# First modulation in column halves, and three weight splits moved, in a two-layer diffusion step on one core

## The chip, the core and the metric

The kernel runs on one core of a Trainium2 chip: TensorE (PE) multiplies, VectorE (DVE), ScalarE (ACT) and GpSimd (POOL) work on its inputs and results, and SyncE (SP) issues the transfers. The metric is the device time of one execution in microseconds (us), lower being better.

## The reference, cut to what matters

Two layers work on 512 latent tokens and 128 context tokens of width 1024. What this change touches is the first half of each layer's normalisation: `shift` and `scale` come from the conditioning, 1024 columns each, and every token is scaled by them before the first projection.

```
mod = (jax.nn.silu(cond) @ lp['w_ada'] + lp['b_ada'])[:, None, :]
sh1, sc1, g1, sh2, sc2, g2 = jnp.split(mod, 6, axis=-1)
h = rmsnorm(x, lp['norm1']) * (1 + sc1) + sh1
proj = h @ lp['w_in']
...
x = x + g1 * y
h = rmsnorm(x, lp['norm2']) * (1 + sc2) + sh2
u = conv3(h @ lp['w_up'], lp['conv_ff'])
```

## The kernel before, in words

Everything is written out by hand, engine by engine, with semaphores; each engine runs its list in order. The tokens lie transposed in `X`: eight tiles `t` of 128 model columns by 644 token columns. Matrices are multiplied in three products of rounded pieces: ScalarE makes the high part of a weight item (`W_hi`, function `item`), GpSimd the rest (`W_lo`, function `low`), and the tokens are split likewise into `H_hi` (ScalarE) and `H_lo` (VectorE). A weight item is 512 KB; there are three slots for raw items and three for split ones.

At a layer's start four things have to meet. **The norm**: ScalarE squares the eight tiles (`square`), VectorE adds them up in `SUM` as they come (`add_square`), TensorE sums over the columns (`first_sums` for `SUM`, `last_sums` for the last square), VectorE and GpSimd make the root (`roots`, `norm_root`), and TensorE spreads it over the partitions (`spread_roots`). **The modulation**: 16 items of `w_ada`, each 128 rows by 1024 columns, eight for `shift` and then eight for `scale`; TensorE multiplies each by the conditioning `CT`, four products of 256 columns that lie on four groups of 32 columns of the array (`ada_products`). Layer 0 takes the items from `AS0` with ten places, layer 1 from places that come free late in layer 0 (`BS_D`, `BS_H`, `BS_N`). When eight are done, ScalarE copies the row sums to `R` (`first_move`), TensorE turns them (`ada_rows`), and VectorE makes `MOD` and the gain `AB`. **The tiles**: for each tile VectorE makes `XN` (`normalise`), ScalarE scales it to `HF` with `MOD` and `AB` and makes `H_hi` (`modulate`), VectorE makes `H_lo` (`norm_rest`). **The first projection**: TensorE takes items 0 to 3 (512 columns, two tiles each, 30 products each), waiting for `H_lo` of each tile and for `W_lo` of each item.

The second norm of a layer does the same without such items in front: its modulation was made during the attention. There GpSimd scales the 128 context columns (`prompt_columns`), and ScalarE splits the third weight of the gated part, item 28 (`NPROJ + NOUT + 2`), between two of its tiles.

Of the kernel before, what the change touches and what calls it, by code (L numbers as in the profile page):

```python
# [313 lines left out]
def backbone_program(nc, x_prompt, x_sample, cache_mla_ckv, cache_mla_kpe, cache_gqa_k, cache_gqa_v,  # L314
# [5 lines left out]
    with ctx:  # L320
# [118 lines left out]
        const_in, c_in, f_in, mask_ok = sem("const_in"), sem("c_in"), sem("f_in"), sem("mask_ok")  # L439
# [40 lines left out]
        def staged(l, x):  # L480

            if l == 0:
                return AS0[:, x % NAS, :], as_in[x % NAS], 16 * (x // NAS + 1)
            return (BS_D[:, x, :] if x < 2 else BS_H[:, x - 2, :] if x < 12 else BS_N[:, x - 12, :]), bs_in[x], 16
# [187 lines left out]
        def _(sp):  # L672
            sp.dma_start(K[:, :], consts).then_inc(const_in, 16)
# [3 lines left out]
            sp.dma_start(CR[0:8, :], c.rearrange("a (k p) -> (a k) p", p=P)).then_inc(c_in, 16)  # L677
            sp.dma_start(CR[8:16, :], c_ctx.rearrange("(k p) -> k p", p=P)).then_inc(c_in, 16)
# [27 lines left out]
            def stage_ada(l, x):  # L706

                if l == 0 and x >= NAS:
                    sp.wait_ge(aw_used, x - NAS + 1)
                rows, landed_, _ = staged(l, x)  # L710
                sp.dma_start(rows, ada_src(l, x)).then_inc(landed_, 16)

            for l in range(DEPTH):
# [36 lines left out]
                if l == 0:  # L750
                    vectors()
                    for x in range(8 * ADA_A):
                        stage_ada(0, x)
                for r in range(NATTADA + NPROJ + NOUT):
# [27 lines left out]
                    if l and r == RAW - 1:  # L782
                        vectors()
                    if r == RAW:
# [42 lines left out]
                if l + 1 < DEPTH:  # L827

                    for x in range(NBS):
                        if x == 2:  # L830
                            sp.wait_ge(w_used, l * NW + (SPL + NW - 4))
                        if x == 12:
                            sp.wait_ge(x_pre, (l + 1) * KT)
# [14 lines left out]
        def _(pool):  # L848
# [6 lines left out]
            pool.wait_ge(const_in, 16)  # L855
# [14 lines left out]
            def prompt_columns(l, t):  # L870
# [5 lines left out]
                elif t == 0:  # L876
                    pool.wait_ge(mod_ok, l * 2 + 2)
# [4 lines left out]
            for l in range(DEPTH):  # L882
# [6 lines left out]
                for s in range(10, NPROJ):  # L889
                    item(l, s)  # L890
                rope_queries(nc.gpsimd, pool, l, 1)
# [7 lines left out]
                for s in range(NPROJ, NPROJ + NOUT + 2):  # L899
# [5 lines left out]
                for s in range(s0, s0 + 4):  # L905
# [11 lines left out]
        def _(act):  # L917
            def copy(dst, src):
# [6 lines left out]
                                 ACT.Silu).then_inc(c_silu, 1)  # L925

# [36 lines left out]
            def first_move(l, sc):  # L963

                act.wait_ge(aw_used, l * (8 * ADA_A) + 8 * sc + 8)
                if sc:
                    act.wait_ge(ada_tr, l * 3 + sc)
                copy(R[:, :], PS[:, sc, 0:256]).then_inc(ada_ev, 1)

            for l in range(DEPTH):  # L970
# [12 lines left out]
                first_move(l, 1)  # L983
                item(l, 0)
                act.wait_ge(mod_ok, l * 2 + 1)
                for t in range(KT):
                    modulate(l * 2, 0, t)
                    if t == 1:
                        item(l, 1)


                for ch in range(len(TOKEN_CHUNKS)):
                    mine = [s_ for s_, item_ in enumerate(TOKEN_ITEMS) if item_[0] == ch]
                    for s_ in mine[2 if ch == 0 else 1:]:
# [185 lines left out]
        def _(pe):  # L1180
# [8 lines left out]
            pe.wait_ge(const_in, 16)  # L1189
            for i in range(TT):  # L1190
# [8 lines left out]
            pe.wait_ge(c_in, 32)  # L1199
            tr(PS[:, 6, 0:16], CR[:, :]).then_inc(c_tr, 1)  # L1200
            pe.wait_ge(f_in, 16)
            tr(PS[:, 7, 0:KT], FR[:, :]).then_inc(f_tr, 1)
            pe.wait_ge(c_silu, 1)
# [3 lines left out]
            def ada_products(k, out, rows, first, last):  # L1207
# [3 lines left out]
                return ins  # L1211

# [56 lines left out]
            for l in range(DEPTH):  # L1269
# [11 lines left out]
                for x in range(8 * ADA_A):  # L1281
                    rows, landed_, value = staged(l, x)
                    pe.wait_ge(landed_, value)
                    ada_products(x % 8, PS[:, x // 8, 0:256], rows, x % 8 == 0, x % 8 == 7).then_inc(aw_used, 1)
                    if l and x == 5:
# [895 lines left out]
```

## Time and profile before

| what | before |
|---|---|
| median of 3 runs | 1748.97 us (1747.81 to 1749.28) |
| profiled execution | 1746.09 us |
| its span | 1744.1 us |
| mean granted TensorE clock | 0.989 of full |
| TensorE busy | 1668.3 us, 96% of the span |
| VectorE, ScalarE, GpSimd busy | 996.5, 590.2, 553.2 us |

The span is what the rows are counted in; 2.0 us of the execution lie around it. TensorE is busy nearly all of the time, so what can be won is where it waits, and it waits at the few places where a norm stands between two projections.

### The profile page before, as it was taken

What the parts mean: (1) busy time and instruction counts of PE and PEld (TensorE: products, weight loads), DVE (VectorE), ACT (ScalarE), POOL (GpSimd) and SP (SyncE); (2) the same over time, 40 slices, a digit from 0 to 9 for tenths busy, and PEclk for the clock granted to TensorE, in tenths of its full rate; (3) what the DMA queues carried; (4) which work ended last, traced back from release to release, by engine and by line L of the source; (5) the groups of instructions that cost most, each with busy time, mean ns of one, the idle gap of its engine ahead of it and who ended that gap; (6) DMA issues with size and microseconds to landing.
All of it is one profiled execution on the core that took longest, in us unless ns stands there. A gap on an engine that the chain in (4) does not pass through costs nothing.

```text
span 1744.1 us, 29770 instructions
## 1 busy us (share of the span) xinstructions
PE 1668.3 (96%) x11742; PEld 1507.7 (86%) x11742; DVE 996.5 (57%) x1604; ACT 590.2 (34%) x1085; POOL 553.2 (32%) x313
## 2 busy tenths in 40 slices
PE   6999988999999999999989999899999999999998
PEld 4888555798999999999968965568899999999997
DVE  4275455237766666666832844541476666666675
ACT  3423444425222222222352234452342222222224
POOL 1354010233433333443325510112333333333332
PEclk8999999999999999999999999999999999999999
DMA  8322520231222222222722344004122222222221
GB/s 325 105 76 79 182 76 1 87 120 49 84 74 72 72 72 72 72 73 73 268 54 80 97 127 149 24 13 157 49 62 79 77 72 72 72 73 79 77 73 61
DMA packets 148449, 156.17 MB, mean 90 GB/s; under 512 B 8280, under 2 KB 118404, under 8 KB 148356
## 3 DMA queue, kind: packets, MB, share of 16 engines
q1 hardware_dynamic: 148356, 154.87, 28.2%
q8 instruction: 66, 1.08, 0.3%
q14 instruction: 27, 0.22, 0.0%
HBM read 151.54 MB, written 3.31 MB: 89 GB/s over the span
## 4 chain that ended last, share of the span: by engine, by line
PE 84%; ACT 5%; DVE 5%; issue 2%; POOL 2%; DMA 1%; SPq 1%; ACTq 0%; DVEq 0%; POOLq 0%
PE PS L1182 79%; PE PS L1186 4%; ACT HF L947 1%; ACT PT L919 1%; POOL SS L887 1%; DMA AS<-in_w_ada_dram 1%; DVE H_lo L1754 1%; ACT PR L1055 1%; ACT H_hi L919 1%; POOL W_lo L859 1%; ACT W_hi L919 0%; DVE CF L2019 0%; DVE X L1780 0%; DVE XN L1747 0%; DVE CF L2022 0%
## 5 line engine op out<-in xcount | busy, mean ns | idle before, releaser
L859 POOL TENSOR_TENSOR W_lo<-RW,W_hi 128x1024 fp32r<-128x1024 f32 (+1 forms) x184 | 482.7, 2632 | 886.2 <-ACT W_hi L919 886.2
L1182 PE MATMUL PS<-H_hi,W_hi 128*128 128x384 f32 x1856 | 576.1, 310 | 10.8 <-DVE H_lo L1754 6.5
L1182 PE MATMUL PS<-H_hi,W_lo 128*128 128x384 f32 x1856 | 576.5, 311 | 0.0
L1182 PE MATMUL PS<-H_lo,W_hi 128*128 128x384 f32 x1856 | 576.0, 310 | 0.0
L1182 PEld LDWEIGHTS PS<-H_hi,W_hi 128*128 128x128 f32 x1856 | 351.7, 190 | 13.4 <-issue 9.5
L1182 PEld LDWEIGHTS PS<-H_hi,W_lo 128*128 128x128 f32 x1856 | 350.4, 189 | 0.0
L1182 PEld LDWEIGHTS PS<-H_lo,W_hi 128*128 128x128 f32 x1856 | 350.3, 189 | 0.1
L919 ACT ACTIVATE W_hi<-RW 128x1024 fp32r<-128x1024 f32 (+1 forms) x184 | 191.3, 1047 | 102.5 <-PE PS L1182 102.5
L1182 PE MATMUL PS<-G_hi,W_hi 128*128 128x384 f32 x704 | 218.8, 311 | 2.2 <-DVE G_lo L2032 2.2
L1182 PE MATMUL PS<-G_lo,W_hi 128*128 128x384 f32 x704 | 218.1, 310 | 0.0
L1182 PE MATMUL PS<-G_hi,W_lo 128*128 128x384 f32 x704 | 217.9, 309 | 0.0
L919 ACT ACTIVATE U<-PS 128x384 f32<-128x384 f32 (+1 forms) x176 | 67.2, 434 | 388.3 <-PE PS L1182 387.9
L2022 DVE SCALAR_TENSOR_TENSOR CF<-U,VT,CF 128x644 f32<-128x644 f32 x88 | 191.1, 2171 | 10.2 <-DVE CF L2019 2.4
L2017 DVE TENSOR_SCALAR CF<-U,VT 128x644 f32<-128x644 f32 x88 | 52.8, 600 | 240.2 <-ACT U L919 239.8
L2019 DVE SCALAR_TENSOR_TENSOR CF<-U,VT,CF 128x644 f32<-128x644 f32 x88 | 134.1, 1524 | 10.9 <-DVE CF L2017 3.7
L2045 DVE TENSOR_TENSOR DN<-PS,DN 128x384 f32<-128x384 f32 (+1 forms) x288 | 120.8, 477 | 26.2 <-PE PS L1182 26.2
L1182 PEld LDWEIGHTS PS<-G_hi,W_hi 128*128 128x128 f32 x704 | 132.8, 189 | 2.6 <-DVE G_lo L2032 2.6
L1182 PEld LDWEIGHTS PS<-G_hi,W_lo 128*128 128x128 f32 x704 | 133.7, 190 | 0.0
L1182 PEld LDWEIGHTS PS<-G_lo,W_hi 128*128 128x128 f32 x704 | 132.6, 188 | 0.0
L919 ACT ACTIVATE G_hi<-CF 128x644 fp32r<-128x644 f32 x44 | 32.7, 743 | 237.4 <-DVE CF L2028 237.4
L1182 PE MATMUL PS<-W_hi,H_hi 128*128 128x512 f32 (+1 forms) x240 | 90.8, 379 | 10.0 <-DVE H_lo L1754 7.4
L919 ACT ACTIVATE PT<-PS 128x512 f32<-128x512 f32 (+1 forms) x102 | 53.8, 576 | 109.9 <-PE PS L1186 105.7
(196 smaller groups left out, 1886.5 us busy)
## 6 DMA issues: line engine op xcount, KB each, us to landing
RW<-in_w_up_dram SPq DMA_DIRECT2D x88, 512.0 KB, 3.7
RW<-in_w_ada_dram SPq DMA_DIRECT2D x48, 512.0 KB, 4.0
RW<-in_w_down_dram SPq DMA_DIRECT2D x44, 512.0 KB, 3.6
RW<-in_w_in_dram SPq DMA_DIRECT2D x28, 512.0 KB, 3.7
AS<-in_w_ada_dram SPq DMA_DIRECT2D x16, 512.0 KB, 11.7
GS<-in_w_ada_dram SPq DMA_DIRECT2D x14, 512.0 KB, 6.9
BS_H<-in_w_ada_dram SPq DMA_DIRECT2D x10, 512.0 KB, 10.1
RW<-in_w_out_dram SPq DMA_DIRECT2D x32, 128.0 KB, 2.8
```

What stands on the lines that cost most here:

```text
L859: nc.gpsimd.tensor_tensor(W_lo[:, slot, 0:width], RW[:, raw, 0:width], W_hi[:, slot, 0:width].bitcast(F32), ALU.subtract).then_inc(w_lo, 1)
L887: nc.gpsimd.tensor_tensor(SS[:, 1, 0:40], SS[:, 0, 0:40], K[:, K_MH:K_MH + 40], ALU.pow).then_inc(hp, 1)
L919: return nc.scalar.activation(dst, src, ACT.Copy)
L947: nc.scalar.activation(HF[:, t % 2, c0:c1], XN[:, t % 2, c0:c1], ACT.Identity, bias=MOD[:, 24 * w + t, cond:cond + 1], scale=AB[:, w, t, c ...
L1055: nc.scalar.activation(prob_ap(step, u), score_ap(step, u), ACT.Exp, bias=stat(step, 0, u), scale=scale, accum_out=stat(step, 1, u)).then_ ...
L1182: return nc.tensor.matmul(out, lhsT, rhs, start=start, stop=stop, skip_group_check=True)
L1186: return nc.tensor.transpose(out, in_, K[0:n, K_ID:K_ID + n])
L1754: v.tensor_tensor(H_lo[:, t, :], HF[:, t % 2, :], H_hi[:, t, :].bitcast(F32), ALU.subtract).then_inc(h_lo, 1)
L2017: v.tensor_scalar(CF[:, ch, s, :], U[:, ch, s, 0:T], column(0), None, ALU.mult).then_inc(cv_own, 1)
L2019: v.scalar_tensor_tensor(CF[:, ch, s, :], U[:, ch, s, 1:T + 1], column(1), CF[:, ch, s, :], ALU.mult, ALU.add).then_inc(cv_own, 1)
L2022: v.scalar_tensor_tensor(CF[:, ch, s, :], U[:, ch, s, 2:T + 2], column(2), CF[:, ch, s, :], ALU.mult, ALU.add).then_inc(cv_done, 1)
L2045: ins = v.tensor_tensor(out, src, out, ALU.add)
```

## The change

It does five things.

1. The 16 items of the first modulation hold 256 rows by 512 columns now. The first eight give `shift` and `scale` of tiles 0 to 3 (half `h` = 0), the last eight those of tiles 4 to 7. A product has 128 columns instead of 256, and an item eight products instead of four (`first_products`).
2. TensorE takes the last eight (`late_products`) after the first projection item in layer 0, and before it in layer 1; `R` is copied and turned for each half apart, and VectorE makes `MOD` and `AB` for four tiles at a time (`first_modulation`). In layer 1 items 10 and 11 are the ones staged first, in `BS_D`.
3. In the list of the norm, the sums stand after the item x = 4 in layer 0 (after 8 before) and after x = 3 in layer 1 (after 1 before); `spread_roots` stands after the eight items. `normalise` of tile 1 moves behind the first `AB`.
4. ScalarE splits projection items 2 and 3 after tiles 3 and 5, no longer after tile 7, and item 28 between the last two squares of the second norm, no longer after its tile 4. GpSimd's list follows.
5. The constants come in five pieces, the identity first and the masks and tables last, behind the late items. The conditioning is loaded second and turned before the tokens, which wait for its Silu; `arrange_masks` moves to the end of the first norm.

```diff
@@ sync: start of the program @@
-            sp.dma_start(K[:, :], consts).then_inc(const_in, 16)
+            constant(K_ID, K_ID + P, const_in)
+            sp.dma_start(CR[0:8, :], c.rearrange("a (k p) -> (a k) p", p=P)).then_inc(c_in, 16)
+            sp.dma_start(CR[8:16, :], c_ctx.rearrange("(k p) -> k p", p=P)).then_inc(c_in, 16)
             for i in range(TT):
                 sp.dma_start(XIN[:, i, :], src).then_inc(x_in[i], 16)
-            sp.dma_start(CR[0:8, :], c.rearrange("a (k p) -> (a k) p", p=P)).then_inc(c_in, 16)
...
+                h, sc, kp = x // 8, x // 4 % 2, x % 4
+                src = w_ada[l, 2 * P * kp:2 * P * (kp + 1), D * sc + 512 * h:D * sc + 512 * (h + 1)]
+                sp.dma_start(rows.rearrange("p (k n) -> p k n", k=2),
+                             src.rearrange("(k p) n -> p k n", p=P)).then_inc(landed_, 16)
...
-                    for x in range(8 * ADA_A):
+                    for x in range(8):
                         stage_ada(0, x)
...
+                    elif r == RAW - 1:
+                        for x in range(8, 16):
+                            stage_ada(0, x)
+                        constant(K_MASK, K_ONE, rest_in)
+                        constant(K_SEL, K_MH, rest_in)
@@ gpsimd @@
-                for s in range(NPROJ, NPROJ + NOUT + 2):
+                for s in range(NPROJ, NPROJ + NOUT + 3):
                     item(l, s)
                 norm_root(l * 2 + 1)
@@ scalar @@
                 first_move(l, 0)
-                first_move(l, 1)
                 item(l, 0)
-                act.wait_ge(mod_ok, l * 2 + 1)
                 for t in range(KT):
+                    if t == 4:
+                        first_move(l, 1)
+                    if t % 4 == 0:
+                        act.wait_ge(mod_ok, l * 3 + 1 + t // 4)
                     modulate(l * 2, 0, t)
-                    if t == 1:
-                        item(l, 1)
+                    if t in (1, 3, 5):
+                        item(l, (t + 1) // 2)
...
                     if t == KT - 2:
                         item(l, NPROJ + NOUT + 1)
+                        item(l, NPROJ + NOUT + 2)
                 for t in range(KT):
                     modulate(l * 2 + 1, 1, t)
-                    if t == 4:
-                        item(l, NPROJ + NOUT + 2)
@@ tensor @@
             pe.wait_ge(const_in, 16)
+            pe.wait_ge(c_in, 32)
+            tr(PS[:, 6, 0:16], CR[:, :]).then_inc(c_tr, 1)
+
+            pe.wait_ge(c_silu, 1)
             for i in range(TT):
...
+            def first_products(l, x):
+                rows, landed_, value = staged(l, x)
+                pe.wait_ge(landed_, value)
+                h, sc, kp = x // 8, x // 4 % 2, x % 4
+                for kk in range(2):
+                    for g in range(4):
+                        ins = mm(PS[32 * g:32 * g + 32, 7 * h, P * sc:P * (sc + 1)], CT[:, 2 * kp + kk, :],
+                                 rows[:, 512 * kk + P * g:512 * kk + P * (g + 1)],
+                                 kp == 0 and kk == 0, kp == 3 and kk == 1)
+                ins.then_inc(aw_used, 1)
...
-                for x in range(8 * ADA_A):
...
+                for x in range(8):
+                    first_products(l, x)
+                    if l and x == 1:
                         pe.wait_ge(x_fin, l * KT + 6)
                         vector_rows()
-                    if x == (1 if l else 8):
+                    if x == (3 if l else 4):
                         first_sums(l * 2)
                         last_sums(l * 2)
...
+                spread_roots(l * 2)
+                ada_rows(l * 6, PS[:, 2, :]).then_inc(ada_tr, 1)
+
+                def late_products():
+                    for x in range(8, 16):
+                        first_products(l, x)
+                if l:
+                    late_products()
...
                     ins.then_inc(w_used, 1)
+                    if s == 0:
+                        if l == 0:
+                            late_products()
+                        pe.wait_ge(ada_ev, l * 6 + 2)
+                        rows_of(PS[:, 7, 256:512], R).then_inc(ada_tr, 1)
@@ vector @@
-                for t in range(2):
-                    normalise(N, t)
+                normalise(N, 0)
...
-            def norm_rest(N):
+            def norm_rest(N, middle=None):
+                normalise(N, 1)
                 for t in range(KT):
+                    if t == 4 and middle:
+                        middle()
                     dve.wait_ge(h_hi, N * KT + (t + 1))
...
+            def first_modulation(l, h):
+                src = PS[:, 7, 256:512] if h else PS[:, 2, 0:256]
+                dve.wait_ge(ada_tr, l * 3 + h + 1)
+                bias = VT[:, 0:16].rearrange("p (o x g b) -> p o x g b", o=2, x=2, b=1)[:, :, h]
...
+                dve.wait_ge(mod_raw, l * 2 + h + 1)
+                gains(0, 4 * h, 4)
...
-                for sc in range(ADA_A):
...
-                gains(l, 0)
-                norm_rest(l * 2)
+                first_modulation(l, 0)
+                norm_rest(l * 2, lambda: first_modulation(l, 1))
+                if l == 0:
+                    arrange_masks()
```

TensorE's list in layer 0, from the first modulation item (`AS,CT`) to the first product of the projection (`W_hi,H_hi`), before. An `x36` counts products, four to an item; `K,NS` is the spread and `K,R` the turned row sums:

```order
L1182 MATMUL PS<-AS,CT 32x256 x36
L1182 MATMUL PS<-K,SUM 128x1 x5
L1182 MATMUL PS<-K,SQ 128x1 x5
L1182 MATMUL PS<-AS,CT 32x256 x12
L1182 MATMUL PS<-K,NS 128x128 x5
L1182 MATMUL PS<-AS,CT 32x256 x4
L1186 MATMUL PS<-K,R 128x128 x2
L1182 MATMUL PS<-AS,CT 32x256 x12
L1186 MATMUL PS<-K,R 128x128 x2
L1182 MATMUL PS<-W_hi,H_hi 128x512
L1182 MATMUL PS<-W_lo,H_hi 128x512
```

The same place after; behind the line of dots stands the end of the first projection item. The `x40` of `32x128` counts products, eight to an item:

```order
L1202 MATMUL PS<-AS,CT 32x128 x40
L1202 MATMUL PS<-K,SUM 128x1 x5
L1202 MATMUL PS<-K,SQ 128x1 x5
L1202 MATMUL PS<-AS,CT 32x128 x24
L1202 MATMUL PS<-K,NS 128x128 x5
L1206 MATMUL PS<-K,R 128x128 x2
L1202 MATMUL PS<-W_hi,H_hi 128x512
...
L1202 MATMUL PS<-W_hi,H_lo 128x512
L1202 MATMUL PS<-AS,CT 32x128 x64
L1206 MATMUL PS<-K,R 128x128 x2
L1202 MATMUL PS<-W_hi,H_hi 128x512
```

Half of the products have left the stretch ahead of the projection, and stand behind its first item in twice the number of pieces.

ScalarE's list in layer 0 from the copy of the row sums, before, through the first four tiles (each is two `HF` and one `H_hi`; rows of further tiles read alike and are left out):

```order
L919 ACTIVATE R<-PS 128x256 x2
L919 ACTIVATE W_hi<-RW 128x1024
L947 ACTIVATE HF<-XN,MOD,AB 128x512
L947 ACTIVATE HF<-XN,MOD,AB 128x128
L919 ACTIVATE H_hi<-HF 128x644
L947 ACTIVATE HF<-XN,MOD,AB 128x512
L947 ACTIVATE HF<-XN,MOD,AB 128x128
L919 ACTIVATE H_hi<-HF 128x644
L919 ACTIVATE W_hi<-RW 128x1024
L947 ACTIVATE HF<-XN,MOD,AB 128x512
```

and after, from its second weight split to the third and on to the copy of the second half's sums:

```order
L937 ACTIVATE W_hi<-RW 128x1024
L966 ACTIVATE HF<-XN,MOD,AB 128x512
L966 ACTIVATE HF<-XN,MOD,AB 128x128
L937 ACTIVATE H_hi<-HF 128x644
L966 ACTIVATE HF<-XN,MOD,AB 128x512
L966 ACTIVATE HF<-XN,MOD,AB 128x128
L937 ACTIVATE H_hi<-HF 128x644
L937 ACTIVATE W_hi<-RW 128x1024
L937 ACTIVATE R<-PS 128x256
L966 ACTIVATE HF<-XN,MOD,AB 128x512
```

The split of item 2 has moved between the tiles, and the copy to `R` for the second half stands before the fifth tile, so that ScalarE waits there for TensorE's late products.

GpSimd's list around the root of the second norm (`NS`), before and after in one piece each:

```order
L638 TENSOR_TENSOR QS<-TC,TD 128x4x32 x2
L859 TENSOR_TENSOR W_lo<-RW,W_hi 128x1024 x10
L867 TENSOR_TENSOR NS<-NS,K 128x5
L878 TENSOR_SCALAR HF<-XN,AB,MOD 128x128 x8
L859 TENSOR_TENSOR W_lo<-RW,W_hi 128x1024 x4
```

```order
L639 TENSOR_TENSOR QS<-TC,TD 128x4x32 x2
L876 TENSOR_TENSOR W_lo<-RW,W_hi 128x1024 x11
L884 TENSOR_TENSOR NS<-NS,K 128x5
L895 TENSOR_SCALAR HF<-XN,AB,MOD 128x128 x8
L876 TENSOR_TENSOR W_lo<-RW,W_hi 128x1024 x3
```

One split of a weight has passed from behind the eight context pieces (`HF`) to ahead of the root.

## Rows read from the trace of the kernel before

**Rows 1.** Timeline of layer 0's start: start us, duration us, engine, line, operation, idle before.
```profile
9.40 4.87 DVE L1691 COPY X<-PS 128x512 f32<-128x512 f32 x8 [0.16 <-PE PS L1186]
13.23 1.28 ACT L924 ACT_TABLE_LOAD   x1 [13.23 <-PE PS L1186]
14.60 1.36 ACT L939 ACTIVATE SQ<-X 128x644 f32<-128x644 f32 x2
...
17.69 4.56 DVE L1723 TENSOR_TENSOR SUM<-SUM,SQ 128x644 f32<-128x644 f32 x5 [0.87 <-ACT SQ L939]
...
23.28 0.64 PE L1182 MATMUL PS<-AS,CT 128*32 128x256 f32 x8 [0.22 <-DMA AS<-in_w_ada_dram]
...
25.11 1.27 PE L1182 MATMUL PS<-K,SUM 128*128 128x1 f32 x10
...
28.39 2.79 PE L1182 MATMUL PS<-AS,CT 128*32 128x256 f32 x24
...
31.11 2.34 PE L1182 MATMUL PS<-K,NS 128*128 128x128 f32 x10
...
34.09 0.28 DVE L1748 TENSOR_TENSOR XN<-X,PS 128x128 f32<-128x128 f32 x1
...
37.22 1.20 ACT L947 ACTIVATE HF<-XN,MOD,AB 128x512 f32<-128x512 f32 x2
...
40.47 0.76 PE L1182 MATMUL PS<-W_hi,H_hi 128*128 128x512 f32 x1 [3.71 <-DVE H_lo L1754]
...
57.03 0.50 PE L1182 MATMUL PS<-W_hi,H_hi 128*128 128x512 f32 x1 [1.08 <-POOL W_lo L859]
```

**Rows 2.** Timeline of layer 1's start, TensorE and one row of ScalarE.
```profile
874.27 1.07 PE L1182 MATMUL PS<-BS_D,CT 128*32 128x256 f32 x16
876.30 1.28 PE L1182 MATMUL PS<-K,SUM 128*128 128x1 f32 x10 [0.96 <-DVE SUM L1723]
...
880.40 2.50 PE L1182 MATMUL PS<-K,NS 128*128 128x128 f32 x10
...
889.64 0.44 PE L1186 MATMUL PS<-K,R 128*128 128x128 f32 x2 [0.50 <-ACT R L919]
...
890.53 1.20 ACT L947 ACTIVATE HF<-XN,MOD,AB 128x512 f32<-128x512 f32 x2
...
893.78 0.76 PE L1182 MATMUL PS<-W_hi,H_hi 128*128 128x512 f32 x1 [3.71 <-DVE H_lo L1754]
...
910.35 0.50 PE L1182 MATMUL PS<-W_hi,H_hi 128*128 128x512 f32 x1 [1.04 <-POOL W_lo L859]
```

**Rows 3.** Timeline of layer 0's second norm.
```profile
389.40 2.40 POOL L859 TENSOR_TENSOR W_lo<-RW,W_hi 128x1024 fp32r<-128x1024 f32 x1 [7.99 <-ACT W_hi L919]
...
395.32 1.18 POOL L867 TENSOR_TENSOR NS<-NS,K 128x5 f32<-128x5 f32 x1 [3.53 <-DVE NS L1731]
...
408.95 1.05 ACT L919 ACTIVATE W_hi<-RW 128x1024 fp32r<-128x1024 f32 x1
...
412.40 0.44 PE L1182 MATMUL PS<-H_hi,W_hi 128*128 128x384 f32 x1 [0.40 <-DVE H_lo L1754]
...
417.31 0.44 PE L1182 MATMUL PS<-H_hi,W_hi 128*128 128x384 f32 x1 [1.09 <-DVE H_lo L1754]
```

**Rows 4.** Timeline of TensorE, 172.7 to 178.6: products of 128 columns on two groups (128*64).
```profile
172.71 0.88 PE L1182 MATMUL PS<-PT,PMG 128*64 128x128 f32 x12
...
177.91 0.66 PE L1182 MATMUL PS<-PT,PMG 128*64 128x128 f32 x8
```

**Rows 5.** Timeline of TensorE, 399.25 to 399.30 alone: what begins in 0.05 us.
```profile
399.26 0.42 PE L1182 MATMUL PS<-GS,CT 128*32 128x256 f32 x4
```

**Rows 6.** Windows: stretch, its length, busy us and instructions by engine, granted clock, DMA.
```profile
28.40:33.40 5.00, 5.00 (x38) 3.15 (x37) 0.17 (x1) 0.00 (x0) 1.17 (x1) 0.53 1.03 406
```

**Rows 7.** The page's DMA issues: count, KB each, median us from issue to landing.
```profile
RW<-in_w_ada_dram SPq DMA_DIRECT2D x48, 512.0 KB, 4.0
RW<-in_w_in_dram SPq DMA_DIRECT2D x28, 512.0 KB, 3.7
```

More of the change, by code:

```diff
@@ L827, in _ @@
                 if l + 1 < DEPTH:
[L829 to L833, printed above, removed]
+                    for x in (10, 11):
+                        stage_ada(l + 1, x)
+                    sp.wait_ge(w_used, l * NW + (SPL + NW - 4))
+                    for x in range(10):
+                        stage_ada(l + 1, x)
+                    sp.wait_ge(x_pre, (l + 1) * KT)
+                    for x in range(12, NBS):
                         stage_ada(l + 1, x)
@@ L904, in _ @@
                 s0 = NPROJ + NOUT + 2
-                for s in range(s0, s0 + 4):
+                for s in range(s0 + 1, s0 + 4):
                     item(l, s)
@@ L961, in ada_move, with first_move @@
                 copy(R[:, :], PS[:, 7, 0:256]).then_inc(ada_ev, 1)
[L963 to L968, printed above, removed]
+            def first_move(l, h):
+                act.wait_ge(aw_used, l * (8 * ADA_A) + 8 * h + 8)
+                if h:
+                    act.wait_ge(ada_tr, l * 3 + h)
+                copy(R[:, :], PS[:, 7 * h, 0:256]).then_inc(ada_ev, 1)
             for l in range(DEPTH):
@@ L1280, in _ @@
                     pe.wait_ge(x_fin, l * KT + 5)
-                for x in range(8 * ADA_A):
[L1282 to L1285, printed above, removed]
+                for x in range(8):
+                    first_products(l, x)
+                    if l and x == 1:
                         pe.wait_ge(x_fin, l * KT + 6)
                         vector_rows()
-                    if x == (1 if l else 8):
+                    if x == (3 if l else 4):
                         first_sums(l * 2)
                         last_sums(l * 2)
-                    if x == (4 if l else 11):
-                        spread_roots(l * 2)
-                    if x == 12:
-                        ada_rows(l * 6, PS[:, 2, :]).then_inc(ada_tr, 1)
-                ada_rows(l * 6 + 1, PS[:, 4, :]).then_inc(ada_tr, 1)
+                spread_roots(l * 2)
[5 more added lines that the diff above has]
+                    late_products()
                 def w_ready(s):
@@ L1696, in _, with arrange_masks @@
             v.memset(X[:, :, T - 2:T], 0.0).then_inc(setup_v, 1)
-            lower, upper = K[:, K_MASK:K_MASK + P], K[:, K_MASK + P:K_MASK + 2 * P]
-            copy(K[:, K_MASK + 3 * P:K_MASK + 4 * P], upper).then_inc(mask_ok, 1)
-            dve.wait_ge(mask_ok, 1)
-            copy(upper, lower).then_inc(mask_ok, 1)
-            dve.wait_ge(mask_ok, 2)
-            v.memset(lower, 0.0).then_inc(mask_ok, 1)
-            dve.wait_ge(mask_ok, 3)
+            def arrange_masks():
+                dve.wait_ge(rest_in, 32)
+                lower, upper = K[:, K_MASK:K_MASK + P], K[:, K_MASK + P:K_MASK + 2 * P]
+                copy(K[:, K_MASK + 3 * P:K_MASK + 4 * P], upper).then_inc(mask_ok, 1)
+                dve.wait_ge(mask_ok, 1)
+                copy(upper, lower).then_inc(mask_ok, 1)
+                dve.wait_ge(mask_ok, 2)
+                v.memset(lower, 0.0).then_inc(mask_ok, 1)
+                dve.wait_ge(mask_ok, 3)
             for n in range(2 * TT):
@@ L1983, in _ @@
                                         ALU.subtract).then_inc(y_lo, 1)
-                gains(l, 1)
+                filled(dve, l, ("AT", 4))
+                gains(1, 0, KT)
                 for t in range(KT):
```

44 lines of the change are left out of this document (22 added, 22 removed).

## The prediction

> **What bounds the kernel now.** I read the page's busy times first: TensorE works 96% of the span, so a change can win only where TensorE waits. The waits of TensorE then lead to four places: the start of each layer and the second norm of each layer. At each I read the timeline, engine beside engine.
>
> In layer 0 TensorE's own order sets the start. `SUM` is complete at 17.69 + 4.56 = 22.25, but the sums stand behind the item x = 8 and begin at 25.11; the items before them come one at a time from memory (x = 7 starts at 23.28 after waiting for its transfer). The spread starts at 31.11, the first tile of `XN` is there at 34.37, and `HF` still waits until 37.22 for the second half of the modulation; the first projection product runs at 40.47, 3.25 after `HF` [rows 1]. In layer 1 all items are on the chip, and TensorE walks the list itself: a wait of 0.96 for `SUM`, the spread at 880.40, the last turned row sums at 889.64 after a wait of 0.50, `HF` at 890.53, the first product at 893.78 [rows 2]. About 15 us after each first product stands a wait of 1.08 and 1.04 for the `W_lo` of item 2 [rows 1, 2]. In the second norm TensorE waits 0.40 and 1.09 for `H_lo` of late tiles, behind ScalarE's split of item 28 at 408.95 (1.05) [rows 3]; layer 1 repeats it.
>
> **The price of an item.** This one number carries the sum, so first that. Two old items in a row take 1.07, one takes 0.64: 0.43 for an item [rows 1, 2]. It holds eight instructions (each product is two), 54 ns each. The four products on the four groups begin within 0.05 us and run together [rows 5], so an item is two such rounds of about 0.215. In attention, twelve and eight instructions of 128 columns on two groups take 0.88 and 0.66: 55 ns each, 110 for a pair that runs together [rows 4]. A new item holds sixteen instructions of 128 columns. If rounds of four take as long as these pairs, it is 4 × 0.11 = 0.44, no more than before. If an instruction costs 55 ns however many groups share the array, it is 16 × 55 ns = 0.88. Rows 5 shows four starting far closer together than 55 ns, so I take 0.48, with 0.43 and 0.88 as ends. In the stretch where the granted clock was 0.53 [rows 6], three items took 2.79, so 0.93 each [rows 1]; I keep that for items that lie there.
>
> The Trainium skill ("TensorE: Matmul & The Clock Gate", Back-to-back issue gap) speaks against the change: in a stream of weight loads and products it gives about 81 ns for a product of 128 columns, which I'd estimate as 16 × 81 ns = 1.30 for a new item. The trace disagrees already, with 54 and 55 ns in such streams; the sum by the page is with the rivals.
>
> **Layer 0, before the first product.** ScalarE's squares begin at 14.60, after Silu, while the tokens are complete at 9.40 + 4.87 = 14.27 [rows 1]. With Silu done ahead of the tokens the squares start up to 0.33 earlier, and `SUM` ends at about 21.92. But the tokens now wait for Silu, and Silu needs the conditioning, its turn and the table load of 1.28 [rows 1]; no row shows how these land when they are issued second. I bound the start of the squares by 1.0 to either side of the value taken, less than one table load. The items come at 406 GB/s [rows 6], 0.52 MB in 1.29 us, so x = 4 is there three items before 23.28, at 19.4, and the sums no longer wait for it. They take 25.11 to 28.39, 3.28, at a low clock: 21.95 to 25.25. Items 5 to 7 follow in 2.8: the spread begins at 28.05. `XN` of the first tile ended 3.26 after the spread began [rows 1]: 31.3. The row sums are copied during the spread and turned right behind it; `MOD` and `AB` come about 0.45 after (889.64 + 0.44 to 890.53 in layer 1 [rows 2]), so `HF` starts at about 31.75 and the first product at 35.0: **5.5 sooner**.
>
> **Layer 0, what is given back.** The late products now stand behind item 0, in TensorE's full stream: 8 × 0.48 = **3.84 later**. Behind them TensorE waits for ScalarE's copy of `R`, 0.50 and 0.44 as at 889.64 [rows 2], **1.0 later**. Queued behind that wait is item 1; ScalarE waits before tile 4 in turn, and GpSimd behind it. Tile 4 is not needed until item 2: the late products end at about 46.6, the copy and turn at 47.55, `H_lo` of tile 4 some 3.7 later at 51.3, and item 2 starts at about 55.3, so this is covered by 4 us. The late transfers, eleven after x = 7 with the three raw weights among them, land at 23.3 + 11 × 1.29 = 37.5, before item 0 ends at about 42.8 (items 0 and 1 took 40.47 to 55.95, 57.03 less the wait [rows 1], so 7.75 each). The wait for `W_lo` goes, since item 2 is split after tile 3: **1.08 sooner**. Layer 0: −5.5 − 1.08 + 3.84 + 1.0 = **−1.7**.
>
> **Layer 1.** The sums stand behind x = 3, so `SUM` is there: 0.96 less. Ahead of the spread there are three items more, 1.44, and the vector rows: from the end of the spread at 882.90 to the wait at 889.14, 6.24 hold eleven items (4.7), turned rows (0.44) and these vector rows, at most 1.1; I take 0.6. The spread begins at 880.40 − 0.96 + 1.44 + 0.6 = 881.5 and ends at 884.0 with its 2.50 [rows 2]; turned rows to 884.4, `HF` at 884.9, the first product at 888.1. The eight late products, 3.84 from 884.4, end at 888.3 and now decide by a hair: 5.5 sooner. The wait of 1.04 goes, 0.44 of turned rows comes behind item 0; `R` for them is copied under that item. Layer 1: **−6.1**. Low clock at the first product (0.76 against 0.50 at 910.35 [rows 2]) could be less with TensorE busy right up to it; I leave that to the range, 1 us.
>
> **Second norms.** The split of item 28 (1.05) moves to where ScalarE waits for the residual. GpSimd's part of it comes behind the one that starts at 389.40, so 389.40 + 2.40 + 2.40 = 394.2, ahead of the root at 395.32 [rows 3]: hidden, by 1.1; with that cover gone each norm would be later by what is over. Both waits go, 0.40 + 1.09 = 1.5 in each layer: **−3.0** (−0.6 to −3).
>
> **Sum.** −1.7 − 6.1 − 3.0 = −10.8. The profiled execution of before was 1746.09 (its span 1744.1 and 2.0 around it), 2.9 under the median of the runs, so it would become 1735.3, and the median 1748.97 becomes **1738.2**. The other edits (order of the constants, masks at the end of the first norm, places of the staged items) cost nothing in it: they lie on the transfer queue behind the items or behind VectorE's work on the norm, and GpSimd waits for them only after its splits of the first projection.
>
> **Rivals.** *A, the item's price follows the number of instructions*, 0.88: 0.40 more for each item. Layer 0 has eleven on the path, x = 5 to 7 at the low clock (2.8 more) and the late eight (3.2 more); layer 1 sixteen (6.4 more). Sum −10.8 + 12.4 = +1.6: 1750.6, no change that can be told. For it: 54 and 55 ns are nearly the same price at 256 and 128 columns. Against it: rows 5. By the skill's 81 ns, an estimate, another 0.42 per item would give about 1762; this is in the chance of the slower side.
> *B, slower: the late transfers*. They read rows of 2 KB in place of 4 KB, and TensorE stands behind item 0 until they land. At the rate of rows 6 they have 42.8 − 37.5 = 5.3 to spare. The 14.2 us of transfers would have to take 14.2 + 5.3 + 10.8 = 30.3 for before's time, a rate of 0.47, and at a third, 42.6, the kernel ends 12 us later: 1761. Against it: weights of the projection, in rows of 2 KB and less, land in 3.7, those of 4 KB in 4.0 [rows 7].
> *C, the second norms gain nothing*, because ScalarE's last square or the root waits for the moved split: −7.8, 1741.2. For it: only 1.1 of cover; the trace has no row of that meeting.
>
> **How the numbers follow.** Forecast 0.62, A 0.13, B and the page's price together 0.11, C 0.14. About 0.2%, 3.5 us, is what a measurement of this kernel can tell from no change. Faster: 0.62 + 0.14 = 0.76; same 0.13; slower 0.11. The range begins at 1734 (items at 0.43, squares 1.0 sooner, 1 us of clock in layer 1, and the scatter of the runs) and reaches to 1746.5, which holds C, squares 1.0 later, and an item price up to about 0.7.
>
> **What would show it.** In layer 0: sums at about 22, spread at about 28, first product near 35, then 128 instructions of late products in about 3.9, a short wait for `R`, and no wait for `W_lo` at item 2. In layer 1 the first product some 14 us after the first item where it was 19.5 (874.27 to 893.78), and no wait ahead of it for `H_lo` above 1 us. In the second norms no wait of TensorE for `H_lo`. The forecast is wrong if an item takes over 0.8, if TensorE waits for a transfer behind item 0, or if the root of a second norm starts later after the last residual.

## The result, and the profile after

| what | after | before, beside it |
|---|---|---|
| median of 5 runs | 1738.11 us (1733.82 to 1739.49) | 1748.97 us (1746.68 to 1749.64) |
| ratio, 95% interval | 0.9939 (0.9926 to 0.9951) | |
| again, on another chip, 6 runs | 1737.55 us, ratio 0.9933 (0.9917 to 0.9948) | 1748.09 us |
| profiled execution, span | 1739.49 us, 1737.3 us | 1746.09 us, 1744.1 us |
| mean granted TensorE clock | 0.987 | 0.989 |
| TensorE busy | 1671.3 us | 1668.3 us |

The kernel is 10.9 us faster by the medians, where 10.8 was forecast. The two profiled executions lie only 6.6 apart: that of before is below all five of its times, that of after is the slowest of its five. So the forecast's total can't be read off the two traces; each of its steps can, and one has to ask each time whether the row is the program's or that execution's. Two executions below (one of the kernel before, one of a variant) took 2057 and 2226 us with a mean granted clock of 0.75 and 0.68, and are left out of every median here.

Layer 0's start after, by the timeline (start us, duration us, engine, line, operation, idle before), answers to [rows 1]:

```profile
15.21 1.37 ACT L958 ACTIVATE SQ<-X 128x644 f32<-128x644 f32 x2 [10.20 <-DVE X L1731]
...
18.31 4.56 DVE L1767 TENSOR_TENSOR SUM<-SUM,SQ 128x644 f32<-128x644 f32 x5 [0.86 <-ACT SQ L958]
...
22.93 2.29 PE L1202 MATMUL PS<-K,SUM 128*128 128x1 f32 x10 [2.44 <-DVE SUM L1767]
25.08 2.27 PE L1202 MATMUL PS<-K,SQ 128*128 128x1 f32 x10
27.29 2.79 PE L1202 MATMUL PS<-AS,CT 128*32 128x128 f32 x48
30.00 2.50 PE L1202 MATMUL PS<-K,NS 128*128 128x128 f32 x10
...
36.94 0.76 PE L1202 MATMUL PS<-W_hi,H_hi 128*128 128x512 f32 x1 [4.00 <-DVE H_lo L1800]
...
45.42 3.70 PE L1202 MATMUL PS<-AS,CT 128*32 128x128 f32 x128
49.63 0.44 PE L1206 MATMUL PS<-K,R 128*128 128x128 f32 x2 [0.50 <-ACT R L937]
```

The order of things is the forecast one: TensorE now waits for `SUM` (2.44), the first product comes at 36.94 where it came at 40.47, the eight late items stand behind item 0, and no wait for `W_lo` follows. 128 instructions take 3.70: 29 ns each, 0.46 an item. The two sums, which took 3.28 with the item ahead of them busy [rows 1], take 4.36 here behind an idle TensorE. The windows of the same trace (length; busy us and instructions of TensorE, its weight loads, VectorE, ScalarE, GpSimd; granted clock; DMA) show the clock: 0.95 while TensorE hardly works (0.07 of 2.00), then 0.50, the lower of the two levels at which the rows run:

```profile
21.00:23.00 2.00, 0.07 (x1) 0.07 (x1) 1.69 (x5) 1.70 (x5) 0.00 (x0) 0.95 1.02 383
23.00:25.00 2.00, 2.00 (x10) 2.00 (x10) 0.00 (x0) 0.12 (x1) 0.00 (x0) 0.50 1.05 407
25.00:27.00 2.00, 2.00 (x11) 2.00 (x11) 0.17 (x1) 0.00 (x0) 0.00 (x0) 0.50 1.05 408
```

Layer 1's start, the same view, answers to [rows 2]:

```profile
872.02 1.08 PE L1202 MATMUL PS<-BS_H,CT 128*32 128x128 f32 x32
...
874.65 1.28 PE L1202 MATMUL PS<-K,SUM 128*128 128x1 f32 x10
875.79 1.96 PE L1202 MATMUL PS<-K,SQ 128*128 128x1 f32 x10
877.68 3.64 PE L1202 MATMUL PS<-BS_H,CT 128*32 128x128 f32 x64
881.25 2.19 PE L1202 MATMUL PS<-K,NS 128*128 128x128 f32 x10
...
888.22 0.47 PE L1202 MATMUL PS<-W_hi,H_hi 128*128 128x512 f32 x1 [0.92 <-DVE H_lo L1800]
```

The wait for `SUM` is gone and the first product stands 16.2 after the first item, against 19.5 before. Four items at 877.68 took 3.64, twice the price: a low clock again (0.50 in the windows from 877 to 881). The product itself takes 0.47, not 0.76: TensorE was busy up to 0.92 ahead of it, and the windows give 1.00 from 885 on.

GpSimd in the second norm of layer 0, ScalarE's moved split, and the one product of TensorE that still waits there, answer to [rows 3]:

```profile
389.17 2.40 POOL L876 TENSOR_TENSOR W_lo<-RW,W_hi 128x1024 fp32r<-128x1024 f32 x1 [7.99 <-ACT W_hi L937]
...
391.56 1.06 ACT L937 ACTIVATE W_hi<-RW 128x1024 fp32r<-128x1024 f32 x1 [2.46 <-PE PS L1202]
...
392.69 2.36 POOL L876 TENSOR_TENSOR W_lo<-RW,W_hi 128x1024 fp32r<-128x1024 f32 x1 [1.12 <-ACT W_hi L937]
395.10 1.19 POOL L884 TENSOR_TENSOR NS<-NS,K 128x5 f32<-128x5 f32 x1
...
402.72 0.41 PE L1202 MATMUL PS<-H_hi,W_hi 128*128 128x384 f32 x1 [1.75 <-DVE H_lo L1800]
```

The waits of 0.40 and 1.09 are gone; the one of 1.75 for the first tile was there before too, at 402.95. The root starts at 395.10 where it started at 395.32, and this whole stretch is 0.22 earlier, so it is not delayed; but the moved piece ends at 392.69 + 2.36 = 395.05, and the cover, the time by which it is done ahead of the root, is 0.05.

### The profile page after: what moved, and what is told of

Read it like the earlier page. It is cut to its first block, busy times and chain, and to the rows that moved or that the text cites. A ratio compares the mean times of both kernels' runs of the same rounds, so it can differ in the third digit from the quotient of the medians.

```text
span 1737.3 us, 30288 instructions
## 1 busy us (share of the span) xinstructions
PE 1671.3 (96%) x11998; PEld 1520.9 (88%) x11998; DVE 999.0 (58%) x1606; ACT 590.7 (34%) x1085; POOL 554.5 (32%) x313
## 4 chain that ended last, share of the span: by engine, by line
PE 88%; DVE 5%; ACT 4%; issue 2%; POOL 1%; DMA 0%; SPq 0%; ACTq 0%; DVEq 0%
PE PS L1202 84%; PE PS L1206 5%; ACT PT L937 1%; ACT PR L1076 1%; POOL SS L904 1%; DVE CF L2072 0%; DVE X L1833 0%; ACT H_hi L937 0%; DVE CF L2075 0%; DVE HO L2017 0%; DVE SUM L1767 0%; ACT HO L937 0%; POOL W_lo L876 0%; DMA XIN<-in_x_sample_dram 0%; ACT PMM L937 0%
## 5 line engine op out<-in xcount | busy, mean ns | idle before, releaser
L2075 DVE SCALAR_TENSOR_TENSOR CF<-U,VT,CF 128x644 f32<-128x644 f32 x88 | 191.0, 2171 | 10.2 <-DVE CF L2072 2.4
L2070 DVE TENSOR_SCALAR CF<-U,VT 128x644 f32<-128x644 f32 x88 | 48.9, 555 | 240.8 <-ACT U L937 240.4
L2072 DVE SCALAR_TENSOR_TENSOR CF<-U,VT,CF 128x644 f32<-128x644 f32 x88 | 138.9, 1578 | 10.3 <-DVE CF L2070 2.4
```

The source lines that it names most:

```text
L2070: v.tensor_scalar(CF[:, ch, s, :], U[:, ch, s, 0:T], column(0), None, ALU.mult).then_inc(cv_own, 1)
L2072: v.scalar_tensor_tensor(CF[:, ch, s, :], U[:, ch, s, 1:T + 1], column(1), CF[:, ch, s, :], ALU.mult, ALU.add).then_inc(cv_own, 1)
L2075: v.scalar_tensor_tensor(CF[:, ch, s, :], U[:, ch, s, 2:T + 2], column(2), CF[:, ch, s, :], ALU.mult, ALU.add).then_inc(cv_done, 1)
```

## The experiments

Medians are given with the ratio to the kernel before on the same chip and its 95% interval. "Faster than the changed kernel" is by its 1738.11 and 1737.55.

**Item 28 alone.** In the kernel before:

```diff
...
                         item(l, NPROJ + NOUT + 1)
+                        item(l, NPROJ + NOUT + 2)
...
-                    if t == 4:
-                        item(l, NPROJ + NOUT + 2)
```

> The kernel before, with only the split of item 28 moved between the last two squares and GpSimd's share ahead of the root. Theory of the prediction: both waits of TensorE in each second norm go (0.40 and 1.09, 0.40 and 1.07) and nothing comes in their place, so 3.0 us less than before and a root that starts where it did, 3.5 us after the start of the last residual add. Rival C: the root or the last square comes later by what GpSimd still has to do, the gain is under 1 us, and the row of the root shows it.

1747.04 against 1749.36, ratio 0.9987 (0.9978 to 0.9996): 2.3 us faster, 0.7 to 3.8. Its trace shows no wait of TensorE for `H_lo` after the first tile, and its GpSimd rows the root right behind the moved piece:

```profile
396.18 2.36 POOL L859 TENSOR_TENSOR W_lo<-RW,W_hi 128x1024 fp32r<-128x1024 f32 x1 [1.12 <-ACT W_hi L919]
398.58 1.19 POOL L867 TENSOR_TENSOR NS<-NS,K 128x5 f32<-128x5 f32 x1
```

The mechanism holds and rival C falls, though "3.5 after the last residual add" now rests on 0.04 of cover. The 3.0 is within the interval. By the rows each norm gives 2.0 (see the second norms in the account below).

**The changed kernel without item 28's move.** Only that move, taken back.

> The changed kernel with only item 28's split back behind tile 4 of the second norms. Theory: the waits of 0.40 and 1.1 come back in both layers, 3.0 us slower than the changed kernel (about 1741), the same as the move was worth alone. Rival: with the other moves it is worth something else, under 1 or over 5 us.

1743.42, ratio 0.9960 (0.9946 to 0.9974). The kernel before had 1749.95 on this chip, more than on the others, so the ratios compare better than the medians: 0.9960 against 0.9939 and 0.9933 is 3.7 to 4.7 us slower than the changed kernel (5.3 and 5.9 by the medians alone). TensorE's timeline has the two waits again:

```profile
414.01 0.44 PE L1203 MATMUL PS<-H_hi,W_hi 128*128 128x384 f32 x1 [0.40 <-DVE H_lo L1801]
...
418.91 0.44 PE L1203 MATMUL PS<-H_hi,W_hi 128*128 128x384 f32 x1 [1.08 <-DVE H_lo L1801]
```

The waits are back as the theory says, and the interval holds its 3.0; the rows make it 2.0 in each layer.

**Splits of items 2 and 3 alone.** In the kernel before:

```diff
-                    if t == 1:
-                        item(l, 1)
+                    if t in (1, 3, 5):
+                        item(l, (t + 1) // 2)
...
```

> The kernel before, with only the splits of items 2 and 3 moved behind tiles 3 and 5. Theory of the prediction: the waits of 1.08 and 1.04 for the low part of item 2 go, 2.1 us faster, and it is the halves that make the splits' old place cost 4.5 in each layer (as seen with the splits put back). Rival: ScalarE's tiles come later by the two splits between them, TensorE waits for H_lo of a late tile instead, and less than 1 us is won.

1749.93 against 1749.95, ratio 0.9996 (0.9985 to 1.0007). In the trace the wait of 1.08 ahead of item 2 is gone, no wait for a late tile has come, and TensorE's wait for `ST` in attention, at 191.94 before, comes at 190.78, 1.16 earlier. So the rival's mechanism is not there in layer 0; but the median does not show the 2.1, and the interval (2.6 faster to 1.2 slower) leaves both theories standing on size. In that execution the root of the second norm comes at 397.99, 2.67 later than before's 395.32; the windows between show a clock of 0.97 where the execution of before had 1.00:

```profile
200.00:300.00 100.00, 89.60 (x722) 56.21 (x719) 50.78 (x122) 43.89 (x122) 7.93 (x27) 0.97 0.21 65
300.00:360.00 60.00, 55.80 (x429) 45.77 (x427) 17.35 (x33) 25.23 (x53) 11.82 (x5) 0.97 0.33 115
```

**All splits back.** The changed kernel with both moves undone (the two diffs above, backwards).

> The changed kernel with all three weight splits back in their old places (items 2 and 3 after tile 7, item 28 after tile 4 of the second norm). If the parts add up as in the prediction's sum, this is 2.1 + 3.0 = 5.1 us slower than the changed kernel, with the waits of about 1 us for the low part of item 2 back in both layers and those of 0.4 and 1.1 in both second norms. Rival: in layer 0 TensorE has the late products between items 0 and 1, which gives ScalarE time, so the wait for item 2 does not come back there and the loss is about 4.

1754.60 against 1749.36, ratio 1.0031 (1.0019 to 1.0042): slower than before. Neither theory had this size. TensorE's timeline has the waits, in both layers:

```profile
62.55 0.50 PE L1203 MATMUL PS<-W_hi,H_hi 128*128 128x512 f32 x1 [4.47 <-POOL W_lo L876]
...
916.59 0.79 PE L1203 MATMUL PS<-W_hi,H_hi 128*128 128x512 f32 x1 [4.49 <-POOL W_lo L876]
```

ScalarE's fifth tile waits for the late modulation, so tile 7, and the split behind it, come later: at 59.03, where the kernel before split at 53.48. The wait for item 2 was 1.08; with halves and the old place it is 4.47, and 4.49 in layer 1, where ScalarE's fifth tile likewise starts after a wait for `AB` (2.06 at 905.59). The parts don't add up: without the moved splits the halves bring waits of 9.0. By the ratios (1.0031 against 0.9960 with item 28 alone put back) the splits of items 2 and 3 are worth 12.4 here; what the rest of it is was not taken apart.

**Old order of loads.** The constants in one piece and the conditioning behind the tokens again:

```diff
-            constant(K_ID, K_ID + P, const_in)
+            constant(0, K_N, const_in)
...
-            pe.wait_ge(c_silu, 1)
             for i in range(TT):
```

> The changed kernel with the constants in one piece, the conditioning behind the tokens and its Silu behind the transposes, as before; the masks stay at the end of the norm. In the changed kernel the squares started at 15.21, not at 14.27 as forecast. Theory: that is the new order's doing (first transposes at 5.36 on a slow TensorE, a wait of 0.75 for the second token tile); here the squares start at about 14.6 again and the kernel is about 0.6 us faster than the changed one, with the first product near 36.3. Rival: something else in the changed kernel holds the tokens, the squares stay at 15.2, and Silu behind them makes this 0.3 us slower.

1738.55, ratio 0.9932 (0.9919 to 0.9945): the same. The squares started at 14.86, but that decides nothing: in ten traces with the new order they start between 13.99 and 16.29 (15.21, 14.83, 14.81, 14.86, 16.29, 14.84, 14.47, 13.99, 14.43, 14.96), in four with the old one between 14.60 and 14.86. Their means are 14.87 and 14.75: the new order brings no earlier start, and more scatter.

**Sums after x = 6 in layer 0.**

```diff
-                    if x == (3 if l else 4):
+                    if x == (3 if l else 6):
```

> The changed kernel with the sums of layer 0 after the item x = 6 in place of x = 4. In the changed kernel TensorE waited 2.44 us for SUM behind x = 4, and then took sums (4.36), three items (2.79) and spread (2.50) all at a granted clock of 0.50. Theory: the position is the sized-wrong step; the items x = 5 and 6 fill the wait, the sums start at about 23.2, run at a higher clock in 2.5 to 3.3, and the spread starts near 27.5 in place of 30.0, so the first product comes 2 to 2.5 us sooner, about 34.6. Rival: the clock falls in the sums whatever stands ahead of them, sums and x = 7 take as long as before, and the spread starts within 1 us of 30.0.

1737.89, ratio 0.9933 (0.9921 to 0.9946): no difference by the median. In the trace:

```profile
23.52 0.64 PE L1202 MATMUL PS<-AS,CT 128*32 128x128 f32 x16 [1.40 <-DMA AS<-in_w_ada_dram]
24.09 1.28 PE L1202 MATMUL PS<-K,SUM 128*128 128x1 f32 x10
25.23 1.89 PE L1202 MATMUL PS<-K,SQ 128*128 128x1 f32 x10
27.05 1.08 PE L1202 MATMUL PS<-AS,CT 128*32 128x128 f32 x16
28.77 2.50 PE L1202 MATMUL PS<-K,NS 128*128 128x128 f32 x10 [0.64 <-POOL NS L884]
```

The first sums are back at 1.28 and both take 2.96 in place of 4.36, with no wait for `SUM` ahead of them. But x = 6 landed late, the spread begins 1.2 sooner, not 2.5, and 0.35 of that is the squares' earlier start. Half of the theory holds; its price does not. With the same position in the two runs with x = 6 and late products ahead, the sums took 1.28 and 1.25 once and 2.29 and 2.27 once, and the old order, where TensorE comes to the sums busy, has the long ones too, in the run with item 28 alone:

```profile
24.83 1.08 PE L1181 MATMUL PS<-AS,CT 128*32 128x256 f32 x8 [0.18 <-DMA AS<-in_w_ada_dram]
25.84 2.29 PE L1181 MATMUL PS<-K,SUM 128*128 128x1 f32 x10
28.00 2.27 PE L1181 MATMUL PS<-K,SQ 128*128 128x1 f32 x10
```

Over all fourteen traces: in the seven in which TensorE waits for `SUM` (0.81 to 3.39) the sums take 2.29 and 2.27 every time, though in two of these the items ahead of the wait ran at the low level already (1.08 each); in the other seven the first sums take 1.27 or 1.28 four times and 2.29 three times. So filling the wait does not always keep the clock, and that the wait lowers it is not shown.

**Late products of layer 1 behind item 0.**

```diff
-                if l:
-                    late_products()
...
-                        if l == 0:
-                            late_products()
+                        late_products()
```

> The changed kernel with the late products of layer 1 behind its first projection item, as in layer 0. Theory: ahead of it they cost nothing, since TensorE waits there for the first tile anyway; behind it they stand in the full stream. The first product stays within 0.5 us of 16 us after the first item, and the kernel is 3.7 us slower by the products, plus up to 1.5 for a first item at low clock. Rival: they do set the first product, which then comes about 2 us sooner, so the loss is under 2 us.

1743.68, ratio 0.9966 (0.9957 to 0.9976): about 5.6 to 6.1 us slower than the changed kernel. The rows:

```profile
888.11 0.77 PE L1202 MATMUL PS<-W_hi,H_hi 128*128 128x512 f32 x1 [5.32 <-DVE H_lo L1797]
...
901.21 0.44 PE L1206 MATMUL PS<-K,R 128*128 128x128 f32 x2 [0.50 <-ACT R L937]
```

The first product waits 5.32 for the first tile where the late products had stood, 13.77 after the first item and not the 16 expected; the changed order has it at 13.80 too where its clock held (the run with x = 6). So ahead of the first product they cost nothing, and behind item 0 their 3.7, a low-clock first item (0.77) and a new wait of 0.50.

**Late products of layer 0 ahead of item 0.** The late items are loaded four behind each of the first two raw weights:

```diff
...
-                if l:
-                    late_products()
+                late_products()
...
-                        if l == 0:
-                            late_products()
```

> The changed kernel with the late products of layer 0 ahead of the first projection item, as in layer 1, and the late items loaded between the raw weights (four behind the first, four behind the second). Theory: in layer 0 the change won little because 3.70 of late products and 0.94 of waiting and turning stand in the full stream, while TensorE waits 4.00 ahead of the first product; there the products fit, the first item no longer runs at a low clock, and the first product comes no more than 0.5 later: 3.5 to 5 us faster than the changed kernel. Rival B in a new place: the late items land after 36.9, TensorE waits for them, and nothing is won or the kernel is slower.

1734.92 (1729.44 to 1737.21), ratio 0.9917 (0.9898 to 0.9935): 2.6 to 3.2 us faster than the changed kernel by the medians, with intervals that overlap. The first product came at 38.18, 1.24 later than in the changed kernel and not the 0.5 at most, after waits for the last two transfers (0.68 and 0.63 at 36.34 and 37.61), and TensorE's wait for `ST` in attention at 187.23, against 191.68 and 192.09 in the two traces of the changed kernel. That row has the 3.5 to 5 of the theory, the medians have less; a little of rival B is there too.

> As the run before, with the sums of layer 0 after x = 6. Theory: the sums after x = 6 bring the first product about 1 to 1.5 us sooner in the trace, and the late items, whose landing does not move, then decide: at most 1 us faster than the run before. Rival: with the sums later TensorE uses items later, places come free later and the late items land later: slower than the run before.

1730.79 over 4 runs, ratio 0.9892 (0.9874 to 0.9911): 4.1 faster than the run before by the medians, where at most 1 was expected. And once more:

> The kernel with all eight late products ahead of the first product of layer 0 and the sums after x = 6 once more, since its first median stands on few times and the version with five of them ahead was not faster than it. Theory: 7 us under the changed kernel was partly the clock; in the trace layer 0 is 2.6 us ahead of it at the first products of the attention, so a ratio to the kernel before of 0.990 to 0.992. Rival: 0.989 or less again, so the gain is the program's.

1733.57 over 4 runs, ratio 0.9904 (0.9887 to 0.9920). The theory's 0.990 to 0.992 holds it. The wait for `ST` stands at 189.05 and 187.00 in these two, no sooner than the 187.23 without x = 6, so no row of layer 0's start answers to the 4.1. These medians lie 4 to 7 us under the changed kernel's and 16 to 17 under before's; whether x = 6 adds to what the place of the late products brings is not settled.

**Five ahead, three behind.** As the last kernel, but `late_products` takes x = 8 to 12 ahead of the first product and the rest behind item 0.

> The kernel with late products ahead of the first product and sums after x = 6, but only the five late items that have landed by then (x = 8 to 12) stand ahead; the last three stand behind item 0. With all eight ahead TensorE waited for four transfers (0.2 to 0.7 each), and the first product came at 39.55 where the first tile was ready at about 34.3. Theory: first product near 35.4, 1.4 of products and 0.9 of waiting and turning behind item 0, so 1.5 to 2 us faster than with all eight ahead, about 1729. Rival: the first item at a low clock again takes 1.5 longer and eats that: no difference.

1736.04, ratio 0.9915 (0.9900 to 0.9929): not faster than with all eight ahead. Its first product came at 37.57, not 35.4: the sums ran at a low clock in this execution (2.29 and 2.27). The rival's reason is not there either: the first item starts at the upper level (0.47). The wait for `ST` is at 188.93, within the 187.00 to 189.05 with eight ahead. By these figures the waits for transfers and the price of standing behind item 0 about cancel.

**The changed kernel again.**

> The changed kernel itself once more, beside the others, since its five times spread over 5.7 us and single effects below are of that size. Both theories: a median between 1736 and 1740. If the spread comes from TensorE's clock, low stretches of 1 to 3 us lie in other places of this trace than in the first one, in the attention too, where the program did not change.

1737.55 (1735.97 to 1739.87). One stretch of layer 1's attention, whose program no part of the change touches, in the windows of the kernel before, the changed kernel and this run:

```profile
1100.00:1150.00 50.00, 41.01 (x330) 27.23 (x329) 27.26 (x65) 25.42 (x72) 7.01 (x24) 1.00 0.00 1
```
```profile
1100.00:1150.00 50.00, 42.88 (x318) 29.29 (x318) 24.91 (x54) 22.94 (x61) 6.30 (x22) 0.90 0.00 1
```
```profile
1100.00:1150.00 50.00, 42.05 (x325) 28.53 (x326) 25.94 (x57) 24.57 (x68) 7.07 (x24) 0.93 0.00 1
```

## Why the prediction was right, step by step

The price of an item was the number on which all hung, and it held: 0.46 (128 instructions in 3.70) where 0.48 was taken. Rival A is out: 29 ns an instruction, not 55. The Trainium skill ("TensorE: Matmul & The Clock Gate", Back-to-back issue gap) gives about 81 ns for such a product in a stream; the trace disagrees, with 29.

*Layer 0, before the first product: mis-sized.* In the profiled execution it came 3.5 sooner, not 5.5. The spread began at 30.00, not 28.05, and two terms of the working make that up: the squares started 0.94 after 14.27, and the sums took 4.36, not 3.28. I had copied the length of the sums from one execution; they have two lengths, in the old order too, and which one comes goes with the clock (all seven traces with a wait for `SUM` have the long one). Of the squares' 0.94, 0.3 is the execution's and 0.6 is not: over ten traces they start at 14.87, so the start up to 0.33 sooner that the new order of loads was to bring is not there. Over six traces with this order of TensorE's list up to the first product (36.94, 36.54, 36.53, 36.58 with the old loads, 38.01, 35.70; mean 36.7) against three of before's (40.47, 42.01, 40.62; mean 41.0) it comes 4.3 sooner.

*Layer 0, what is given back: right in mechanism*, 3.70 for the products and 0.7 for wait and turn (49.63 less 0.50 to the next product 0.19 behind), where 3.84 and 1.0 were taken. The tiles behind the late modulation were covered as worked out, and the late transfers were there. The wait for `W_lo` went; but the runs without the splits showed that I had valued that move too low, at 2.1, by the wait that it removed. In the changed kernel it also keeps out 3.4 more in each layer. And the wait of 1.08 is itself one execution's: in the run with item 28 alone, whose layer 0 is the old one, item 0 ran at the low level for longer (0.63 a product up to 47.70, against 43.17), and item 2 did not wait. As a whole, layer 0's start can be read at TensorE's wait for `ST` in attention, before and after:

```profile
191.94 1.09 PE L1182 MATMUL PS<-K,ST 128*64 128x128 f32 x16 [0.35 <-DVE ST L1945]
```
```profile
191.68 1.09 PE L1202 MATMUL PS<-K,ST 128*64 128x128 f32 x16 [0.35 <-DVE ST L1997]
```

Two traces with the old layer 0 have it at 191.94 and 193.59, four with the new one at 191.68, 192.09, 193.20 and 191.19: by the means 0.7 sooner, where 1.7 was forecast.

*Layer 1: right, with a size that the clock sets.* 5.5 sooner was forecast, 3.3 in the profiled execution. The forecast had the first product some 14 after the first item, and three traces have it at 13.80, 13.81 and 14.32; over ten traces with the late products ahead there it is 13.8 to 16.2, mean 15.3, over three of before's 19.5, 21.2 and 19.6, mean 20.1: 4.8. I had priced x = 4 to 7 at full clock behind the sums, and in the profiled execution they took 3.64, the low clock's price. The late products were to decide by a hair; they don't: TensorE waits another 0.92 for the first tile behind them.

*Second norms: right in mechanism, too low in size.* TensorE's last sums before the norm came 0.22 earlier than before in layer 0 and layer 1's first item 2.25 earlier, so 2.0 was won between; 1.49 of that are the two waits, and the other 0.5 was not taken apart. The same 2.0 stands in all fourteen traces. From the root to layer 1's first item they take 478.9 or 477.5 with the split in its old place, 476.9 or 475.6 with it moved; from layer 1's second root to the end 494.8 to 494.9 or 493.4 to 493.6, and 492.7 to 493.2 or 491.4 to 491.6. The longer of each pair has the slower spread (`K,NS`). The cover of 1.1 that I gave GpSimd was wrong: ScalarE's split had to wait until 391.56 for a slot that TensorE freed, which I did not follow, and the cover is 0.05. It was enough.

*The sum.* With the means over traces in place of one execution, layer 0 is −4.3 − 1.1 + 3.7 + 0.7 = −1.0, layer 1 −4.8 − 1.0 + 0.4 = −5.4 and the second norms −2.0 each: −10.4 against 10.9 and 10.5 by the medians. That 1738.2 was met to 0.1 owes something to luck: layer 0 won 1.0 (0.7 by `ST`) in place of 1.7 and layer 1 5.4 in place of 6.1, and the second norms made it up with 4.0 in place of 3.0.

*What is argued only.* It is argued, not shown, that the two profiled executions differ by 6.6 and not by the medians' 10.9 because of low clock. Two stretches hold the difference. From layer 1's second root to the end the pair has 493.58 and 492.83, 0.75 apart in place of 2.0: the spread took 1.38 before and 2.37 after. From layer 1's first item to that root it has 376.25 and 372.45, 3.80 apart, where nine traces of the new order lie at 366.25 to 372.45, mean 370.5. In this stretch the windows show 0.90 over 50 us of the changed kernel where before has 1.00; an estimate from the instructions done in it, 318 in place of 330, makes that about 2 us. It was not taken apart further. What decides in which stretch the clock falls stays open.

## What to carry to other kernels

When a stretch of work is halved so that the next stage can start on one half, put the other half where the engine waits anyway, not behind the first item of a full stream: in layer 1 that place was free, in layer 0 it took back 4.4 of 5.4 won, and moving it brought another 3 to 7 us (the larger with the sums moved too, on few executions). Look also at what stands behind the tiles that now wait for the second half; with three weight splits left in their old places the change was 5 us slower than before in place of 11 faster, and two of them stood behind such tiles. And a duration copied from one trace of the old kernel is that execution's: look for a second trace before a sum rests on it.

## What the runs showed that was not expected

TensorE's granted clock falls to half in stretches that the program does not touch, in some executions and not in others: from 1100 to 1150 us it was 1.00, 0.90 and 0.93 in three traces, from 200 to 300 us 1.00 in the profiled executions of both kernels and 0.97 in the run with the splits of items 2 and 3 alone. In the first of these stretches the changed kernel has 0.50 from 1130 to 1135 and 1.00 from 1137.5 on. One program's times spread by 5.7 us; how much of that is the clock was not shown (1739.00 came with a mean of 0.990, 1733.82 with 0.989). So effects of 1 to 2 us were read from rows, and not from medians.

Two tiny sums of ten instructions each took 1.28 and 1.25 or 2.29 and 2.27, with the clock, and the items on four groups have two prices as well: one more in a row adds 0.43 (two take 1.07 or 1.08, one 0.64) or 0.86 (three take 2.79, one 1.08). Eight instructions of 256 columns and sixteen of 128 cost the same at either level of the clock; three items took 2.79 in both kernels where it was low.
